# Second attention of a two-block network on one core: one VectorE operation a head for mask, scale and minimum, reciprocals copied wide, meta weights gathered, two steps reordered

## The reference

```python
def sink_softmax(sc, sink):
    m = jnp.maximum(jnp.max(sc, axis=-1, keepdims=True), sink)
    e = jnp.exp(sc - m)
    return e / (jnp.sum(e, axis=-1, keepdims=True) + jnp.exp(sink - m))

def swa_layer(x, norm_g, w_in, w_out, sinks, k_sh, v_sh, cos, sin):
    q, gate = jnp.split(rms_norm(x, norm_g) @ w_in, 2, axis=-1)
    q = partial_rope(q.reshape(B, L, B_Q_HEADS, B_HEAD_DIM), cos, sin)
    o = swa_sink_attention(q, k_sh, v_sh, sinks)
    return x + (o * jax.nn.silu(gate)) @ w_out
```

## Time and profile before

| what | us |
|---|---|
| median of 3 runs (2384.24 to 2388.14) | 2384.89 |
| the profiled execution | 2390.32 |
| its span in the trace | 2388.6 |
| TensorE busy in the span | 2304.6 (96%) |
| VectorE busy | 1603.4 (67%) |
| ScalarE busy | 1130.2 (47%) |
| GpSimd busy | 97.2 (4%) |

### The profile page before, as it was taken

How to read it: one execution, slowest core, us unless ns; L and a number is a source line. 1 busy time by engine, 2 the same in 40 slices (tenths; PEclk the granted TensorE clock), 3 DMA queues, 4 the chain that set the end, 5 groups by cost and what they waited for, 6 DMA issues and landing times.

```text
span 2388.6 us, 34521 instructions
## 1 busy us (share of the span) xinstructions
PE 2304.6 (96%) x13343; PEld 2003.1 (84%) x13343; DVE 1603.4 (67%) x1973; ACT 1130.2 (47%) x1693; POOL 97.2 (4%) x182
## 2 busy tenths in 40 slices
PE   6889999999899999999999999999999999999897
PEld 5678888887688888888888889999999999778786
DVE  6877677777768865666656676667667555666654
ACT  3355444443365543555345554444454445455443
POOL 0000100011100000000000000000000000000000
PEclk8889999999999999999999999999999999999999
DMA  9999788798757755555655655444444545433352
GB/s 353 372 362 359 239 278 270 240 320 316 274 193 251 266 188 192 182 188 176 201 188 176 218 172 174 144 142 142 143 140 143 176 152 161 145 106 107 106 194 106
DMA packets 229910, 492.95 MB, mean 206 GB/s; under 512 B 9618, under 2 KB 12392, under 8 KB 226696
## 3 DMA queue, kind: packets, MB, share of 16 engines
q1 hardware_dynamic: 210384, 432.05, 53.5%
q0 software_dynamic: 14144, 50.93, 6.4%
q10 hardware_dynamic: 5256, 8.20, 1.0%
HBM read 488.49 MB, written 2.10 MB: 205 GB/s over the span
## 4 chain that ended last, share of the span: by engine, by line
PE 83%; DVE 7%; DMA 5%; issue 2%; ACT 2%; SPq 0%; POOL 0%; POOLq 0%; DVEq 0%; ACTq 0%
PE ps L1748 32%; PE ps L1766 21%; PE ps L1781 14%; PE ps L1783 7%; DMA ada<-in_ada_w 3%; PE ps L2225 2%; DVE wlo L1055 2%; DMA raw<-in_a_w_in 2%; PE ps L2052 1%; DVE acc L1064 1%; PE ps L2195 1%; ACT whi L547 1%; PE ps L1892 1%; ACT eb__133 L965 1%; PE ps L2071 1%
## 5 line engine op out<-in xcount | busy, mean ns | idle before, releaser
L1055 DVE TENSOR_TENSOR wlo<-raw,whi 128x1024 fp32r<-128x1024 f32 x720 | 872.8, 1222 | 516.3 <-ACT whi L547 514.5
L547 ACT ACTIVATE whi<-raw 128x1024 fp32r<-128x1024 f32 x720 | 756.0, 1057 | 835.4 <-PE ps L1748 410.4
L1781 PE MATMUL ps<-xt__59,whi 128*128 128x512 f32 x1408 | 498.8, 399 | 0.9 <-DVE h L1247 0.7
L1783 PE MATMUL ps<-xt__59,wlo 128*128 128x256 f32 x1408 | 395.4, 281 | 0.0
L1748 PE MATMUL ps<-whi,xt__59 128*128 128x512 f32 x1024 | 334.6, 404 | 17.4 <-DVE xt__59 L1167 17.4
L1766 PE MATMUL ps<-xmh__60,whi 128*128 128x272 f32 x1088 | 322.6, 297 | 3.8 <-DVE ks L1452 3.1
L1781 PEld LDWEIGHTS ps<-xt__59,whi 128*128 128x128 f32 x1408 | 264.7, 188 | 67.6 <-DVE h L1247 2.2
L1766 PE MATMUL ps<-xmh__60,wlo 128*128 128x272 f32 x1088 | 315.0, 289 | 0.0
L1766 PE MATMUL ps<-xml__61,whi 128*128 128x272 f32 x1088 | 313.1, 288 | 0.0
L1783 PEld LDWEIGHTS ps<-xt__59,wlo 128*128 128x128 f32 x1408 | 266.1, 189 | 0.1
L1748 PEld LDWEIGHTS ps<-whi,xt__59 128*128 128x128 f32 x1024 | 198.9, 194 | 60.0 <-DVE xt__59 L1167 14.0
(11 more groups left out here) (297 smaller groups left out, 3287.5 us busy)
## 6 DMA issues: line engine op xcount, KB each, us to landing
raw<-in_a_w_in SPq DMA_DIRECT2D x128, 1024.0 KB, 5.3
raw<-in_ffn_w_up SPq DMA_DIRECT2D x88, 1024.0 KB, 5.0
ada<-in_ada_w POOLq DMA_DIRECT2D x96, 512.0 KB, 4.5
raw<-in_a_w_out SPq DMA_DIRECT2D x48, 1024.0 KB, 5.9
raw<-in_ffn_w_down SPq DMA_DIRECT2D x44, 1024.0 KB, 5.1
mods<-in_ada_w SPq DMA_DIRECT2D x64, 512.0 KB, 10.9
raw<-in_b_w_in SPq DMA_DIRECT2D x32, 1024.0 KB, 5.5
ada<-in_ada_w SPq DMA_DIRECT2D x16, 1024.0 KB, 10.5
```

The source lines that it names most:

```text
L547: act.activation(whi[:, r % 4], raw[:, r // 2, r % 2], ACT.Copy).then_inc(hi_ready, 1)
L1055: dve.tensor_tensor(wlo[:, r % 4], raw[:, r // 2, r % 2], whi[:, r % 4].bitcast(F32), ALU.subtract).then_inc(lo_ready, 1)
L1781: pe.matmul(both, whi[:, r % 4, i, c * P:c * P + P], xt_[:, :, k * T:k * T + T], start=first and i == 0, stop=last and i == 1, skip_group_ ...
L1783: mm = pe.matmul(ps[:, bank + c, 0:T], wlo[:, r % 4, i, c * P:c * P + P], xth[:, k, :], start=False, stop=last and i == 1, skip_group_chec ...
```

## The change

On VectorE, the five operations of step a+4 become four `tensor_tensor_reduce` (one a head: add the mask, scale by minus one eighth, minimum, started from minus the sink) and one small addition; ScalarE waits for each head by itself, with `scale=-1.0`, and does the sink's exponential behind the four. The reciprocal is taken of 128x4 and copied to 128x256. `ob` moves from step a+7 to a+8 and stands in front of step a+5; `rr` moves to the front of `quad_act`; `gb` moves from t%8 = 3 to t%8 = 2. GpSimd gathers the exponentials of the 16 meta keys of four heads into `ebm`, 128x128 with zeros between; one transpose, one copy of 128x128 (`wtm`) and two matmuls of 128 columns with `vbd` (the meta values laid out in blocks) take the place of four transposes, one copy of 16x512 and two matmuls of 256 columns. `vbd` is zeroed and filled by four DMAs of GpSimd, which count on `kd_ready`, so that its waits go from 64 to 128. The wait for `b_o` moves from the transposes to the product with the values.

```diff
@@ gpsimd, behind the four kd DMAs
+            pool.memset(vbd[:, :, :, :], 0.0).then_inc(sem("pool_own"), 1)
+            pool.memset(ebm[:, :], 0.0).then_inc(sem("pool_own"), 1)
+            pool.wait_ge(sem("pool_own"), 9)
+            pool.wait_ge(sem("vb_ready"), 1)
+            for i in range(4):
+                pool.dma_start(vbd[32 * i:32 * i + NM, :, i // 2, i % 2 * BH:i % 2 * BH + BH],
+                               vb[0:NM, 1, :].rearrange("p (j d) -> p j d", d=BH)).then_inc(sem("kd_ready"), 16)
+            for n in range(16):
+                pool.wait_ge(sem("b_exp"), 4 * n + 4)
+                if n:
+                    pool.wait_ge(sem("b_wturned"), n)
+                pool.tensor_copy(ebm[:, :].rearrange("p (i m) -> p i m", m=32)[:, :, 0:NM],
+                                 eb_[:, :, P:P + NM]).then_inc(sem("b_meta"), 1)
@@ quad_act
+                for n in quads(t, 7):
...
                 for n in quads(t, 4):
                     nk = (144, L)[n // 2 % 2]
-                    act.wait_ge(sem("b_max"), n + 1)
-                    act.activation(st[:, 136:140], st[:, 132:136], ACT.Exp).then_inc(sem("b_sexp"), 1)
                     for i in range(4):
-                        act.activation(eb_[:, i, 0:nk], sb_[:, i, 0:nk], ACT.Exp, bias=st[:, 128 + i:129 + i],
+                        act.wait_ge(sem("b_max"), n * 4 + i + 1)
+                        act.activation(eb_[:, i, 0:nk], sb_[:, i, 0:nk], ACT.Exp, bias=st[:, 128 + i:129 + i], scale=-1.0,
                                        accum_out=st[:, 140 + i:141 + i]).then_inc(sem("b_exp"), 1)
+                    act.wait_ge(sem("quad_own"), n * 4 + 1)
+                    act.activation(st[:, 136:140], st[:, 132:136], ACT.Exp).then_inc(sem("b_sexp"), 1)
                 for n in quads(t, 6):
                     act.wait_ge(sem("b_wturned"), n + 1)
-                    for kb in range(2 + n // 2 % 2):
...
+                    for kb in (0, 2) if n // 2 % 2 else (0,):
+                        act.activation(wtb[:, kb], ps[:, TURN_BANK[kb], :].rearrange("p (i q) -> p i q", q=P), ACT.Copy)
+                    act.activation(wtm[:, :], ps[:, 7, 0:P], ACT.Copy).then_inc(sem("b_wt"), 1)
-                for n in quads(t, 7):
...
@@ quad_dve
-                    own6(dve.scalar_tensor_tensor(out=s, in0=ps[:, 4:8, 0:nk], scalar=BH ** -0.5,
...
-                    own6(dve.tensor_reduce(st[:, 120:124], s, AX.X, ALU.max))
-                    own6(dve.tensor_tensor(st[:, 124:128], st[:, 120:124], sink, ALU.max))
-                    own6(dve.tensor_scalar(st[:, 128:132], st[:, 124:128], -1.0, None, ALU.mult))
-                    dve.tensor_tensor(st[:, 132:136], sink, st[:, 124:128], ALU.subtract).then_inc(sem("b_max"), 1)
+                    for i in range(4):
+                        dve.tensor_tensor_reduce(out=sb_[:, i, 0:nk], in0=ps[:, 4 + i, 0:nk], in1=maskB[:, tok, 0:nk],
+                                                 scale=-BH ** -0.5, scalar=nsink[:, h0 + i:h0 + i + 1], op0=ALU.add,
+                                                 op1=ALU.min, accum_out=st[:, 128 + i:129 + i]).then_inc(sem("b_max"), 1)
+                    dve.wait_ge(sem("b_max"), n * 4 + 4)
+                    own6(dve.tensor_tensor(st[:, 132:136], sinkb[:, h0:h0 + 4], st[:, 128:132], ALU.add))
-                for n in quads(t, 5):
...
-                    own6(dve.reciprocal(rb[:, :, :], st[:, 144:148].unsqueeze(2).broadcast_to([P, 4, BH])))
-                for n in quads(t, 7):
+                for n in quads(t, 8):
...
+                for n in quads(t, 5):
...
+                    own6(dve.reciprocal(st[:, 148:152], st[:, 144:148]))
+                    if n:
+                        dve.wait_ge(sem("b_o"), n)
+                    own6(dve.tensor_copy(rb[:, :, :], st[:, 148:152].unsqueeze(2).broadcast_to([P, 4, BH])))
...
-                if n >= 4 and t % 8 == 3:
+                if n >= 4 and t % 8 == 2:
                     gb(n - 4)
                 if n >= 4:
                     quad_dve(t)
@@ quad_pe
-                    for kb in (0, 2, 1) if tok else (0, 1):
+                    for kb in (0, 2) if tok else (0,):
                         kc, w = BLK[kb]
-                        if n and kb == 1:
-                            pe.wait_ge(sem("b_o"), n)
                         for i in range(4):
-                            mm = pe.transpose(ps[0:w, TURN_BANK[kb], i * P:i * P + P], eb_[:, i, kc:kc + w], ident[:, :])
+                            pe.transpose(ps[:, TURN_BANK[kb], i * P:i * P + P], eb_[:, i, kc:kc + w], ident[:, :])
+                    pe.wait_ge(sem("b_meta"), n + 1)
+                    mm = pe.transpose(ps[:, 7, 0:P], ebm[:, :], ident[:, :])
                     mm.then_inc(sem("b_wturned"), 1)
                 for n in quads(t, 3):
...
+                    if n:
+                        pe.wait_ge(sem("b_o"), n)
+                    else:
+                        pe.wait_ge(sem("kd_ready"), 128)
-                    for kb in range(2 + tok):
...
+                    for kb in (0, 2) if tok else (0,):
                         for e in range(2):
...
+                    for k in range(2):
+                        mm = pe.matmul(ps[:, 3, k * P:k * P + P], vbd[:, j, k, :], wtm[:, :], start=False, stop=True,
+                                       skip_group_check=True)
@@ scalar, t = 11; the same at the tensor engine, t = 12
-                        act.wait_ge(sem("kd_ready"), 64)
+                        act.wait_ge(sem("kd_ready"), 128)
```

More of the change, by code:

```diff
@@ L309, in program @@
         sinkb = place("sinkb", [P, 32], O_ACC + 7424)
+        vbd = place("vbd", [P, 4, 2, P], O_ACC + 8 * KB)
+        ebm = place("ebm", [P, P], O_ACC + 13 * KB + 512)
+        wtm = place("wtm", [P, P], O_ACC + 13 * KB)
+        nsink = place("nsink", [P, 32], O_ACC + 7808)
         tabq = place("tabq", [P, 2, 2, 16], O_ACC + 7552)
@@ L1615, in quad_dve @@
                     j, tok, half = n // 4, n // 2 % 2, n % 2
-                    own6 = Own(dve, sem("quad_own"), n * 6)
+                    own6 = Own(dve, sem("quad_own"), n * 4)
                     nk = (144, L)[tok]
                     dve.wait_ge(sem("b_scores"), n + 1)
-                    s = sb_[:, :, 0:nk]
-                    sink = sinkb[:, j * 8 + 4 * half:j * 8 + 4 * half + 4]
-                    own6(dve.scalar_tensor_tensor(out=s, in0=ps[:, 4:8, 0:nk], scalar=BH ** -0.5,
-                                                  in1=maskB[:, tok:tok + 1, 0:nk].broadcast_to([P, 4, nk]),
-                                                  op0=ALU.mult, op1=ALU.add))
-                    own6(dve.tensor_reduce(st[:, 120:124], s, AX.X, ALU.max))
-                    own6(dve.tensor_tensor(st[:, 124:128], st[:, 120:124], sink, ALU.max))
-                    own6(dve.tensor_scalar(st[:, 128:132], st[:, 124:128], -1.0, None, ALU.mult))
-                    dve.tensor_tensor(st[:, 132:136], sink, st[:, 124:128], ALU.subtract).then_inc(sem("b_max"), 1)
-                for n in quads(t, 5):
[L1629 to L1634, removed]
-                    own6(dve.reciprocal(rb[:, :, :], st[:, 144:148].unsqueeze(2).broadcast_to([P, 4, BH])))
-                for n in quads(t, 7):
+                    h0 = j * 8 + 4 * half
+                    for i in range(4):
+                        dve.tensor_tensor_reduce(out=sb_[:, i, 0:nk], in0=ps[:, 4 + i, 0:nk], in1=maskB[:, tok, 0:nk],
[4 more added lines that the diff above has]
+                for n in quads(t, 8):
                     j, tok, half = n // 4, n // 2 % 2, n % 2
@@ L1644, in quad_dve @@
                        .then_inc(sem("b_o"), 1)
+                for n in quads(t, 5):
+                    own6 = Own(dve, sem("quad_own"), n * 4 + 1)
+                    dve.wait_ge(sem("b_sexp"), n + 1)
+                    dve.wait_ge(sem("b_exp"), n * 4 + 4)
+                    own6(dve.tensor_tensor(st[:, 144:148], st[:, 140:144], st[:, 136:140], ALU.add))
+                    own6(dve.reciprocal(st[:, 148:152], st[:, 144:148]))
+                    if n:
+                        dve.wait_ge(sem("b_o"), n)
+                    own6(dve.tensor_copy(rb[:, :, :], st[:, 148:152].unsqueeze(2).broadcast_to([P, 4, BH])))
             def rope_q(j, tok):
@@ L1907, in u_chunk @@
                     pe.wait_ge(mod_added, mod_adds(3, 7) + 16)
[L1908 removed]
+                    row_all(0, "mod_spread")
                 else:
@@ L2249, in _ @@
                     pe.wait_ge(sem("vb_ready"), 1)
-                    pe.wait_ge(sem("kd_ready"), 64)
+                    pe.wait_ge(sem("kd_ready"), 128)
                 if t == Q_TURN_AT[0]:
```

42 lines of the change are left out of this document (18 added, 24 removed).

## The result

| | before | after |
|---|---|---|
| median, us | 2384.56 (2383.66 to 2388.14, 4 runs) | 2366.48 (2365.02 to 2368.28, 4 runs) |
| profiled execution, us | 2390.32 | 2365.02 |
| second attention in the trace, us | 247.76 | 228.57 |

The ratio is 0.9922, with a 95% interval of 0.9908 to 0.9937.

The account below looks back on a forecast made before the run. TensorE, busy 96% of the span, was taken as the bound. -6.9 - 1.4 - 0.3 - 0.3 - 0.5 - 1.7 - 1.65 + 5.1 = -7.65 us, from the median 2384.89 to 2377.2 us; range 2369 to 2383.

Parts of the forecast that it names:

- TensorE's own work: Transposes and values in every quad: 0.43 us less a quad, 6.9 us in all, bounds 4.3 and 9.9 us.
- Quad 2 and unit 32: TensorE's stalls for late exponentials and for qx go with the shorter way to the exponentials: -1.4 and -0.3 us.
- Quad 3: Values waiting for weight copies: shorter copies make the stall 1.9 instead of 2.2 us, -0.3 us; clock falls as before.
- Quad 9: Transposes behind gb(0): stall 1.35 us instead of 1.83, -0.5 us; clock stays up, -1.7 us.
- Quad 11: Values behind gb(1): stall 2.85 us instead of 4.50, -1.65 us; clock falls as before.
- Quad 14: Transposes, with gb(2) now in front: new stall of 3.6 us plus 3.5 us of clock, net +5.1 us.
- The clock: TensorE's granted clock after stalls: falls as before behind quads 3 and 11, none behind 9 (-1.7 us), 3.5 us behind 14.
- The added waits: b_o move, kd_ready at 128 and the gather: no cost with the median DMA landing of 3.5 us.
- rival 2: vbd DMAs land at 6.6 us, qx 2.6 us later with 3 us of clock: 2382.8 us; chance 0.12.
- Rival 1: Matmul pair costs half a key block (3.0 us), quad 14's stall spares the clock (3.5 us): 2370.7 us; chance 0.12.
- Rival 3: GpSimd's gather meets a lo in quads 1, 9 and 14, 1.0 us each, 3.1 together: 2380.3 us; chance 0.05.
- Rival 4: VectorE's one-head operation is expensive, 1.86 us for 272 keys, costing 19 us: 2396 us; chance 0.08.

Follow-up runs that it names:

- f3: Changed kernel with gb behind quad_dve, quad_act ahead of pair_out (t = 27) and gate_out (from t = 43), quad 9's heads ahead of gb(0): 2356.91 us, ratio 0.9878.
- e9: f3 with the gather undone, the 16-key block transposed, copied and multiplied as before: 2360.9 us, ratio 0.9893.
- e2: Changed kernel with only gb put back at t%8 = 3: 2361.81 us, ratio to before 0.9901.
- f1: Changed kernel with gb still at t%8 = 2 but behind quad_dve: 2363.9 us.
- e3: Changed kernel without the gather and vbd, 16-key block handled as before, ob at step a+7: 2381.94 us, ratio to before 0.9978.
- e8: e3 with the 16-key block transposed and multiplied at full height of 128 rows, padded with zeros: 2373.47 us, ratio to before 0.9942.
- e1: The changed kernel run once more, unchanged: 2367.6 us.
- e5: Changed kernel with one more 128x128 copy on ScalarE in front of wtm, in quads 3 and 11 alone: 2367.2 us.
- f2: Changed kernel with ScalarE's quad_act in front of pair_out at t = 27 and of gate_out from t = 43: 2361.3 us.
- e4: Changed kernel with the five operations on four heads back in place of one operation a head: 2378.10 us, ratio to before 0.9971.
- e6: Changed kernel with the reciprocal of 128x256 back in place of 128x4 and its copy: 2364.7 us, ratio to before 0.9904.
- e7: Changed kernel with the old places of rr and ob back, gb as changed: 2370.0 us, ratio to before 0.9920.

## Why the prediction was wrong, point by point

The direction and the places were right; the sum was short by more than half, and two thirds of what was missing lie in one term.

- **TensorE's own work.** Predicted 6.9 us with bounds of 4.3 and 9.9; f3 against e9 gives 8.3 for the gather, and the table 9.6 between before and after (226.0 and 216.4). The pair of matmuls took 0.64 us and saved the identity pair 0.19, as weighed. What I left out: in a quad of 272 keys the change of height between blocks goes too, so the two key blocks take 1.01 us and not 1.16. Right mechanism, one size off. The other 1.3 us between before and after I can't assign.
- **The stalls.** Predicted 12.2 us before and 9.7 after in the four places; measured 12.9 (with three short ones that I left out) and 8.9. Quad 2 and unit 32: gone, as predicted. Quad 3: 1.92 for 1.9. Quad 9: 1.08 for 1.35, since one head of 144 keys took 0.37 us. Quad 11: 2.58 for 2.85, near in size, but not for the reason I gave: I put it down to `gb` one step earlier, and e2 shows the same 2.58 with `gb` in its old place. Which part brought it stays open, so that the size came out is luck. Quad 14: 3.36 for 3.6, a new stall, as predicted, and e2 and f1 confirm that it is the move of `gb` that makes it.
- **The clock: the step that failed.** I took the loss behind a stall from the rows of before, 3.4 and 3.6 us, and carried it over: "and I add 3.5 us for the clock, as behind quads 3 and 11". Quad 9's fall I took away. That made 8.7 us before into 10.5 after. Measured are 8.9 and 3.2. Behind quad 3 that is 1.7 us for 3.4, behind quad 11 nothing for 3.6, and behind quad 14 1.5 for 3.5. The rows of before do not carry over, because the change takes out the 16-row blocks around the stalls. Without these blocks, 16 of the 26 stalls of 1.9 to 3.4 us in all profiles were followed by a fall, and each fall cost 1.5 to 1.7 us. With them (before and e3) all six stalls of 1.8 to 4.5 us were; five of these falls cost 2.9 to 3.8 us, and the one behind quad 9 of before 1.65. That the blocks bring the price down is shown by e8 against e3; why quad 11 had no fall at all is not. The sentence on the stall of 1.37 us was right as far as it went, since no stall up to 1.53 us was followed by a fall in any profile. But length does not decide above that: after 2.58 us it stayed up in after, and after 1.92 us it fell. This term is 7.5 us of the 11.5 that are missing in the stretch; own work of the gather is 1.4, the stalls 1.4, and 1.3 us I can't assign.
- **The added waits.** The `vbd` DMAs landed in 4.6 to 4.9 us, between the bounds, and the first of the two `qx` copies waited 1.2 us for them:

```profile
2027.49 1.26 ACT L1005 ACTIVATE qx<-ps,st 128x512 f32<-128x512 f32 x2 [1.22 <-DMA vbd<-vb]
```

  TensorE's stall in front of unit 10 was 0.78 us in both kernels, so it cost nothing in this execution. In e1 it was 1.20, and in the ten profiles with `vbd` 0.78 to 1.35, while all four without it (before, e3, e8, e9) have 0.78. So the late values cost at most 0.6 us, where rival 2 had 2.6 and the clock. This wait lies in front of the stretch.
- **The rivals.** Rival 1 (a larger gain) came nearest, with both of its halves in part: 1.4 of 3.0 us in own work, and a cheaper fall behind quad 14. It failed in that I gave it quad 14's clock alone, when the same holds for all. Rival 3: TensorE never waited for GpSimd. By the rule of the Trainium skill (SBUF — State Buffer, "Who interferes with whom") a VectorE instruction with two SBUF inputs contends with a GpSimd instruction that reads SBUF. The trace agrees: the three gathers that began inside such an operation took 0.38 to 0.68 us and not 0.24. They were those of quads 7, 12 and 13, and not of 1, 9 and 14; none of them met a `lo`, and TensorE did not ask for them that soon. So the order that the prediction relied on held, and the rival failed. Rival 4: the head's operation costs 1.8 ns an element with its fixed part, not 6.8.
- **The parts of the change.** Undone one at a time they cost 14.6 us (gather), 8.9 (one operation a head), -5.1 (`gb`), and nothing (reciprocals, order of `rr` and `ob`, whose stretches are 1.5 us shorter by one fall of the clock less) in the stretch. The first three sum to 18.4 of 19.2 us. That this is so near is in part luck, since the share of the clock depends on which stalls are followed by a fall.

## What to carry to other kernels

Where TensorE bounds, list its stalls one by one with what each waits for, and price an edit by the stalls that it touches; before, ScalarE waited 74.7 us for the maximum, while all stalls of TensorE together were 12.9 us. A read that waits for the end of a chunk belongs behind all work that does not need that chunk, on its own engine and on the engine that follows it: four such places cost 12 us in the changed kernel. And the clock's share must not be carried over from the kernel before when the change alters the matmuls around a stall: bound it from nothing to the rows.

## What the runs showed of the hardware

- The same stall of 3.36 us cost 1.5 to 1.7 us of clock in seven profiles without 16-row blocks (after, e1, e5 to e8, f2) and 2.9 us in the one with them (e3). With these blocks padded with zeros, at the same count of matmuls and columns, the loss over the stretch fell from 9.7 to 3.4 us and the kernel became 8.5 us faster.
- Without a stall the blocks of 16 rows left the clock at 1.00 (e9).
- A stall of 6.05 us cost 2.9 us of clock without 16-row blocks (e4).
- Among kernels with nearly the same stalls the number of falls was one to three of four (e5, e6, e7, e8). What decides that stayed open.
- Among the key blocks of the values, going from 128 rows to 16 and back costs about 0.15 us each time (1.74 against 1.45 us for two changes, 1.16 against 1.01 for one; e3 and e8).
- A GpSimd copy of 128x64 took 0.24 us, and 0.38, 0.62 and 0.68 us where it began inside an operation of VectorE with two SBUF inputs (after).
- An operation of VectorE with an accumulated minimum shows as two instructions, 497 and 83 ns for 272 elements, and four of them follow each other by 0.42 us.
